# Suffix sums of stick-breaking attention: one fp32 matmul in place of a high and a low fp32r matmul

## What is computed

```python
def block(args):
    qblk, n = args
    z = jnp.einsum('bhqd,bshd->bhqs', qblk, kf) * (dh ** -0.5)
    qpos = n * BLK + jnp.arange(BLK)
    causal = kpos[None, :] < qpos[:, None]
    sp = jnp.where(causal, jax.nn.softplus(z), 0.0)
    after = lax.cumsum(sp, axis=3, reverse=True) - sp
    a = jnp.where(causal, jnp.exp(jax.nn.log_sigmoid(z) - after), 0.0)
    return jnp.einsum('bhqs,bshd->bqhd', a, vf)
```

## Time and profile before

| | |
|---|---|
| median of 3 runs | 2264.76 us |
| lowest and highest | 2262.39 and 2268.1 us |
| the profiled execution, its time | 2263.29 us |
| the profiled execution, its span | 2261.4 us |
| granted TensorE clock, mean | 0.998 |
| PE busy | 2225.7 us (98%) |
| DVE busy | 1328.7 us (59%) |
| ACT busy | 1084.7 us (48%) |
| PE's share of the chain that ended last | 89% |

### The profile page before, as it was taken

The page is one execution under the profiler, slowest core; times in us unless marked ns, Lnnn a source line. Parts: engine busy times, 40 slices in busy tenths (PEclk is TensorE's granted clock), DMA queues, the critical chain, the costliest instruction groups (busy, mean ns, idle before and its releaser), DMA issues.

```text
span 2261.4 us, 26415 instructions
## 1 busy us (share of the span) xinstructions
PE 2225.7 (98%) x10756; PEld 1825.0 (81%) x10756; DVE 1328.7 (59%) x1658; ACT 1084.7 (48%) x1340; POOL 18.1 (1%) x53
## 2 busy tenths in 40 slices
PE   8999999999999899999999999999999999999999
PEld 6888878888888678888888878878887888888887
DVE  5446575456545864556556766765556545666545
ACT  5444564445444654445444453454445444565433
POOL 0000000000000000000000000000000000000000
PEclk9999999999999999999999999999999999999999
DMA  8564546555654356547564544536565654546553
GB/s 290 185 189 149 173 134 207 189 187 186 209 182 149 131 175 204 177 145 235 178 207 137 184 141 136 189 113 222 177 195 173 214 189 155 168 149 204 176 187 109
DMA packets 212937, 401.45 MB, mean 178 GB/s; under 512 B 12368, under 2 KB 30928, under 8 KB 212688
## 3 DMA queue, kind: packets, MB, share of 16 engines
q1 hardware_dynamic: 212816, 399.76, 54.0%
HBM read 398.66 MB, written 1.05 MB: 177 GB/s over the span
## 4 chain that ended last, share of the span: by engine, by line
PE 89%; DVE 5%; ACT 2%; DMA 2%; issue 1%; POOL 0%; SPq 0%; ACTq 0%; DVEq 0%; POOLq 0%
PE ps L1102 26%; PE ps L1103 25%; PE ps L1104 25%; PE ps L1145 4%; DVE wl L771 2%; PE ps L1210 1%; PE ps L1209 1%; PE ps L1208 1%; ACT wh L499 1%; DMA raw<-in_ffn_w_in 1%; DMA raw<-in_ple_w_gate 1%; PE ps L1326 1%; PE ps L1429 1%; PE ps L1345 1%; DMA raw<-in_swa_w_out 0%
## 5 line engine op out<-in xcount | busy, mean ns | idle before, releaser
L771 DVE TENSOR_TENSOR wl<-raw,wh 128x1024 fp32r<-128x1024 f32 x730 | 867.1, 1222 | 479.8 <-ACT wh L499 475.1
L499 ACT ACTIVATE wh<-raw 128x1024 fp32r<-128x1024 f32 x730 | 752.6, 1058 | 595.1 <-PE ps L1104 416.0
L1102 PE MATMUL ps<-wh,xh 128*128 128x512 f32 x2064 | 813.0, 394 | 4.7 <-DVE xl L778 4.7
L1104 PE MATMUL ps<-wh,xl 128*128 128x512 f32 x2064 | 803.5, 389 | 0.0
L1103 PE MATMUL ps<-wl,xh 128*128 128x512 f32 x2064 | 803.2, 389 | 0.0
L1102 PEld LDWEIGHTS ps<-wh,xh 128*128 128x128 f32 x2064 | 388.7, 188 | 86.1 <-DVE xl L778 6.4
L1104 PEld LDWEIGHTS ps<-wh,xl 128*128 128x128 f32 x2064 | 388.3, 188 | 81.3
L1103 PEld LDWEIGHTS ps<-wl,xh 128*128 128x128 f32 x2064 | 388.8, 188 | 76.6
L1102 PE MATMUL ps<-wh,hth 128*128 128x512 f32 x736 | 289.1, 393 | 2.0 <-DVE htl L784 2.0
L1104 PE MATMUL ps<-wh,htl 128*128 128x512 f32 x736 | 286.8, 390 | 0.0
L1103 PE MATMUL ps<-wl,hth 128*128 128x512 f32 x736 | 286.5, 389 | 0.0
(11 more groups left out here) (109 smaller groups left out, 1118.4 us busy)
## 6 DMA issues: line engine op xcount, KB each, us to landing
raw<-in_ffn_w_in SPq DMA_DIRECT2D x352, 512.0 KB, 4.7
raw<-in_ffn_w_out SPq DMA_DIRECT2D x176, 512.0 KB, 4.4
raw<-in_dil_w_in SPq DMA_DIRECT2D x72, 512.0 KB, 4.4
raw<-in_sb_w_in SPq DMA_DIRECT2D x48, 512.0 KB, 4.6
raw<-in_ple_w_gate SPq DMA_DIRECT2D x32, 512.0 KB, 4.8
raw<-in_sb_w_out SPq DMA_DIRECT2D x16, 512.0 KB, 5.0
gb<-in_ln_g SPq DMA_DIRECT2D x12, 512.0 KB, 6.0
gb<-in_ln_b SPq DMA_DIRECT2D x12, 512.0 KB, 6.6
```

The lines of the kernel that those rows point to most:

```text
L499: act.activation(wh[:, u % RING, :], raw[:, u % RAWS, :], ACT.Copy).then_inc(hi_done, 1)
L771: dve.tensor_tensor(wl[:, u % RING, :], raw[:, u % RAWS, :], wh[:, u % RING, :].bitcast(F32), ALU.subtract).then_inc(lo_done, 1)
L1102: pe.matmul(out_, a_h, b_h, start=start, stop=False)
L1104: return pe.matmul(out_, a_l, b_h, start=False, stop=stop)
```

## The change

The suffix sums take `ssp` itself and the fp32 constants, in one fp32 matmul where there were two fp32r matmuls. The rounding and the subtraction on DVE, the tiles `sph`, `spl`, `lower_r` and `ones_r`, and two of ACT's four copies of constants are gone. In `cum` the product with `ones` of one head now follows that head's product with `lower`.

```diff
-        lower_r = sb("lower_r", [P, P], F32R)
-        ones_r = sb("ones_r", [P, P], F32R)
...
-        sph, spl = (v.rearrange("p c t m -> p (c t m)").rearrange("p (b h n) -> p b h n", b=2, h=2) for v in (hth, htl))
...
-                    act.activation(lower_r[:], const("lower"), ACT.Copy).then_inc(masks_done, 1)
-                    act.activation(ones_r[:], const("ones"), ACT.Copy).then_inc(masks_done, 1)
...
                 def soft(hh, h):
                     dve.wait_ge(ln_done.sem, ln_done.at(i, hh, h))
-                    own(dve.scalar_tensor_tensor(ssp[:, h % 2], zpair(h), 0.0, sw[:, h % 2], ALU.max, ALU.add))
-                    own(dve.tensor_copy(sph[:, h % 2], ssp[:, h % 2]))
-                    dve.tensor_tensor(spl[:, h % 2], ssp[:, h % 2], sph[:, h % 2].bitcast(F32), ALU.subtract).then_inc(sp_done.sem, 1)
+                    dve.scalar_tensor_tensor(ssp[:, h % 2], zpair(h), 0.0, sw[:, h % 2], ALU.max, ALU.add).then_inc(sp_done.sem, 1)
...
                 def cum(hh, h):
                     pe.wait_ge(sp_done.sem, sp_done.at(i, hh, h))
                     for m in range(2):
-                        for of in (sph, spl):
-                            pe.matmul(zpair(h)[:, m, :], lower_r[:], of[:, h % 2, m, :], start=False, stop=False, skip_group_check=True)
-                    for m in range(2):
-                        for of in (sph, spl):
-                            ins = pe.matmul(zpair(h)[:, m, P:2 * P], ones_r[:], of[:, h % 2, m, 2 * P:3 * P], start=False,
-                                            stop=of is spl, skip_group_check=True)
+                        pe.matmul(zpair(h)[:, m, :], const("lower"), ssp[:, h % 2, m, :], start=False, stop=False, skip_group_check=True)
+                        ins = pe.matmul(zpair(h)[:, m, P:2 * P], const("ones"), ssp[:, h % 2, m, 2 * P:3 * P], start=False,
+                                        stop=True, skip_group_check=True)
                     ins.then_inc(cum_done.sem, 1)
...
-                    pe.wait_ge(masks_done, 4)
+                    pe.wait_ge(masks_done, 2)
```

## The result

| | before | after |
|---|---|---|
| median of 12 runs | 2264.07 us | 2271.54 us |
| lowest and highest | 2262.39 and 2268.45 us | 2269.05 and 2274.05 us |
| ratio, 95% interval | | 1.0028 [1.0019, 1.0036] |
| the profiled execution, its time and span | 2263.29 and 2261.4 us | 2269.05 and 2267.1 us |
| PE busy, DVE busy | 2225.7 and 1328.7 us | 2235.2 and 1306.0 us |

The kernel became slower, by 7.5 us between the medians and 6.3 us by the ratio. The forecast was 2272.5 us (2267 to 2278), with +7.7 us by its sum.

The account below looks back on a forecast made before the run. PE, busy for 98% of the span, was taken to bound the kernel. Longer cum pieces, less the waits ended at cum(2), gave +3.85 us a layer, +7.7 us for two: 2272.5 us against the median, range 2267 to 2278.

Parts of the forecast that it names:

- the four waits: PE at cum(2) waits for soft's last step on DVE, 1.6 us in all; claimed to go with the shorter soft.
- The low bound: A cum in PE's stream: 4 x 0.32 + 4 x 0.11 = 1.72 us at least, +6.9 us in all.
- high bound: A cum with fp32r's overhead on all eight records, up to 0.013 us more each: 1.82 us, +8.5 us in all.
- two nearest rows: Trace rows pricing a full-size fp32 record: z and av's fp32 records (0.32 us for 384 columns), cum's fp32r record (0.175).
- The pair: cum(0) and cum(1) back to back, up to av(0): +1.32 us in the first half, +1.25 in the second.
- the piece around cum(2): Last record before cum(2) to second record after it: 2.27 us becomes 0.23 + 1.77 + 0.23, -0.08 for both halves.
- Leaving for av: Last short fp32 record of a cum before av: 0.22 us, 0.10 more than within the stream.
- Counting passes alone: Skill's rule of four passes for fp32: 2048 more columns, 0.84 us a cum, 13.4 us for 16.
- Exposed weight loads: Rival: weight loads of full-size fp32 matmuls not hidden, 0.11 us more a record, +21.8 us, 2286.6; chance 0.05.
- Streaming at the fp32r rate: Rival: full-size fp32 record takes 0.175 us, only the four waits count, 2.3 us gained, 2262.5; chance 0.06.
- The remaining wait: Rival: cum(2) still waits as long as now, 2.3 us more, +10.0, 2274.8 us; chance 0.07.
- The first two rivals: Wait remaining at cum(2), chance 0.07, and exposed weight loads, chance 0.05; together said to add 0.11 to slower.

Follow-up runs that it names:

- run 1: Changed kernel's four fp32 matmuls in cum, with DVE still rounding and subtracting before it signals; 2274.45 us against 2264.63 for the kernel before, ratio 1.0042.
- run 2: Kernel before with its eight fp32r matmuls, DVE writing the softplus once in fp32r, low part left out; 2261.75 us against 2264.63, ratio 0.9986.
- run 5: Changed kernel with each fp32 product with lower taken twice; 2289.92 us against 2265.4 for the kernel before, ratio 1.0107.
- Run 3: Kernel before with only the product with ones in fp32, lower still in two fp32r parts; 2264.83 us against 2264.63, ratio 1.0000.
- Run 4: Kernel before with only the product with lower in fp32, ones still in two fp32r parts; timed once, 2274.3 us beside a median of 2265.4.
- run 8: Kernel before with both weight units ahead of cum(2), ACT taking weights(3) first, and the softplus low part and its constants in bf16; 2260.27 us against 2265.4, ratio 0.9975.

## Why the prediction was right

**The bound and the sign.** PE's stream sets the time in this stage. Taking 25 us of work from DVE gained about 2.7, the four waits; adding to PE's stream cost all that was added, or nearly all (runs 1, 2 and 5). The wait at cum(2) went with 1.07 us to spare (the prediction said 1.0), and nothing took its place.

**The term of the stream.** The low bound of 1.72 us was nearly the measured value: 0.32 and 0.11 us for a record, 1.73 us for a cum, where I took 1.77. The 0.015 us that an fp32r record shows above its column rate is not there in a full-size fp32 record. (The prediction works out 0.015 and then adds 0.013 for each of eight records; with 0.015 its high bound would have been 1.84 and not 1.82. Nothing hangs on it.) Of the two nearest rows the one of the same type (z and av, two side by side in part of the array) gave the price, and the one of the same shape did not. The pair came out at 3.56 (forecast 3.64), cum(3) at 1.82 (1.87), the piece around cum(2) at 2.19 (2.23); the sum of the pieces is +7.1 where the forecast had +7.7, inside its +6.9 to +8.5. Leaving for av cost as forecast. That the medians differ by 7.5 us, nearer to the forecast 7.7 than the pieces are, is luck of the scatter; the ratio gives 6.3.

**Two readings that were off.** The prediction lays the longer pair of the second half (2.39 against 2.32 us) to av(0) waiting for weights(0). Kernel before, second record of cum(1) in the first half, and first two in the second half:

```profile
245.76 0.33 PE L1429 MATMUL ps<-htl,lower_r 128*128 128x384 f32 x1
...
288.46 0.44 PE L1429 MATMUL ps<-hth,lower_r 128*128 128x384 f32 x1
288.74 0.34 PE L1429 MATMUL ps<-htl,lower_r 128*128 128x384 f32 x1
```

From cum(1)'s second record to av(0) it is 1.00 us in the first half (245.76 to 246.76) and 1.01 in the second (288.74 to 289.75), so av(0) is not held. The difference stands ahead of it: cum(1)'s first record takes 0.28 us (288.46 to 288.74) and not 0.23 (245.53 to 245.76). Why it does so in one half only no run shows. The sum took the whole piece from the trace, and in the changed kernel both pairs are 3.56 us, so the +1.25 came near (+1.17) all the same. The other reading is the price of a wait: 4 x 0.57 = 2.3 us left out the slow first record behind it, and runs 1 and 2 show 0.67 to 0.68 us for each, 2.7 in all. That price stands in the rivals only; the sum for cum(2) was built from its parts and did not need it.

**Passes and records.** Counting passes alone would have given +13.4 us for the stream. A cum grew by 0.64 us (1.09 to 1.73) where that count gives 0.84. Run 3 shows where most of the difference lies: of the four short fp32r records three already took 0.11 us each, which is what a short fp32 record takes. Run 4 shows the other side, 0.59 us for a cum in the product with lower alone, near 4 x (0.32 - 0.175) = 0.58. That it is the weight load that holds the short records is supported, not shown, by run 8.

**The rivals.** Exposed weight loads would have made records of 0.43 us; they are 0.32. Streaming at the fp32r rate would have made 0.175. The remaining wait needs the long soft (run 1).

**The chances.** The first two rivals have 0.07 and 0.05, so they add 0.12 to slower and not 0.11. 0.66 stood on slower by over 0.3%, and the ratio is 1.0028 [1.0019, 1.0036], on the line and by its centre just under it. The sum of the pieces, 7.1 us, is 0.31%; at this size the scatter of whole executions decides on which side of 0.3% the ratio falls, and two thirds was somewhat sure of itself for a sum that was itself 0.6 us too high.

## What to carry to other kernels

An fp32 matmul in place of a high and a low fp32r matmul takes as many records at half the rate: here it was free where the records are short (128 columns, ratio 1.0000 [0.9991, 1.0009]) and cost 0.15 us a record at 384 columns, so count by the record's step and not by passes. If the work that it saves lies on an engine that nobody waits for but in one place, cover that place with work that is already there; here moving one weight unit ahead, and then one on ACT, gained what the shorter chain did without its price. After such a move look for the next engine's order behind it, as the wait of av(3) showed.

## What was not expected of the hardware

A full-size fp32 record streamed at 0.32 us for 384 columns without the 0.015 us above the column rate that each fp32r record of the same shape carries. Behind the start of the last short fp32 record of a cum the next fp32r record's start stands 0.03 us later and the one after it another 0.31 us (255.38 and 255.69), in place of 0.11 and 0.23: the sum is the same, only where the record's start stands differs. So steps at a change of kind are to be read in pairs. The same goes for bf16 and fp32r: 0.04 us from a bf16 record to an fp32r one, 0.14 to 0.31 us from an fp32r record to a bf16 one (run 8).
